# Six products of the identity behind the scores of five levels of a gated recurrence

## The reference

```python
def _hgrn2(q, k, log_f, v, s0):
    ...
    def step(S, inp):
        qc, kc, gc, vc = inp
        b = jnp.cumsum(gc, axis=2)
        diff = jnp.where(tri, b[:, :, :, None, :] - b[:, :, None, :, :], -jnp.inf)
        a = jnp.einsum('bhnmd,bhnd->bhnm', jnp.exp(diff) * kc[:, :, None, :, :], qc)
        o = jnp.einsum('bhnm,bhmv->bhnv', a, vc) + jnp.einsum('bhnd,bhdv->bhnv', qc * jnp.exp(b), S)
        bl = b[:, :, -1:, :]
        S = jnp.exp(bl[:, :, 0, :, None]) * S + jnp.einsum('bhmd,bhmv->bhdv', kc * jnp.exp(bl - b), vc)
        return S, o
    ...
```

## Time and profile before

| | us |
|---|---|
| median of 3 runs (lowest, highest) | 3379.21 (3378.7, 3379.85) |
| the profiled execution, its own time | 3380.08 |
| its span in the trace | 3378.3 |
| TensorE matmul busy in the span | 3088.4 (91%) |
| VectorE, ScalarE, GpSimd busy | 1558.7 (46%), 531.7 (16%), 1058.3 (31%) |
| mean granted TensorE clock | 0.935 of full |

### The profile page before, as it was taken

One profiled execution on the slowest core, in us unless ns is written; L12 is line 12 of the kernel. 1 busy time (PEld: TensorE's weight loads), 2 busy tenths in 40 slices (PEclk: granted clock), 3 DMA queues, 4 the chain that ended last, 5 costly groups with the idle time before them and its releaser, 6 DMA issues. The chain is left out here.

```text
span 3378.3 us, 43932 instructions
## 1 busy us (share of the span) xinstructions
PE 3088.4 (91%) x18135; PEld 2937.9 (87%) x18135; DVE 1558.7 (46%) x1786; ACT 531.7 (16%) x874; POOL 1058.3 (31%) x551
## 2 busy tenths in 40 slices
PE   7997668899999999999988879689979999999999
PEld 6987468789999999998977769469869999999999
DVE  4152454256626436256114444663446634626343
ACT  3111122152000000002111021351252000000000
POOL 3332033114334334343320142103203434434342
PEclk9998679999999999999986789789989999999999
DMA  3111121401111111113100111011221111111112
GB/s 117 44 31 38 24 90 56 142 24 50 45 48 44 39 49 40 47 38 99 41 19 14 46 56 38 15 67 49 87 101 47 48 40 50 37 50 44 44 44 80
DMA packets 274509, 175.86 MB, mean 52 GB/s; under 512 B 15262, under 2 KB 261406, under 8 KB 274398
## 3 DMA queue, kind: packets, MB, share of 16 engines
q1 hardware_dynamic: 274398, 174.29, 16.9%
HBM read 158.00 MB, written 16.27 MB: 52 GB/s over the span
## 5 line engine op out<-in xcount | busy, mean ns | idle before, releaser
L327 PE MATMUL psum<-moving_hi,w_hi 128*128 128x384 f32 (+1 forms) x3888 | 1285.4, 331 | 71.9 <-PEq L515 24.9
L328 PE MATMUL psum<-moving_lo,w_hi 128*128 128x384 f32 (+1 forms) x3888 | 1279.3, 329 | 0.0
L329 PE MATMUL psum<-moving_hi,w_lo 128*128 128x384 f32 (+1 forms) x3888 | 1279.3, 329 | 0.0
L289 POOL TENSOR_TENSOR w_hi<-w_raw,one 128x1024 fp32r<-128x1024 f32 (+2 forms) x236 | 407.1, 1725 | 1934.2 <-PE psum L329 1390.3
L327 PEld LDWEIGHTS psum<-moving_hi,w_hi 128*128 128x128 f32 x3888 | 739.6, 190 | 79.9 <-issue 63.7
L328 PEld LDWEIGHTS psum<-moving_lo,w_hi 128*128 128x128 f32 x3888 | 739.8, 190 | 0.5 <-issue 0.5
L329 PEld LDWEIGHTS psum<-moving_hi,w_lo 128*128 128x128 f32 x3888 | 739.1, 190 | 0.0
L294 POOL TENSOR_TENSOR w_lo<-w_raw,w_hi 128x1024 fp32r<-128x1024 f32 (+2 forms) x236 | 574.0, 2432 | 18.5
L368 DVE TENSOR_TENSOR residual<-psum,residual 128x768 f32 x192 | 130.1, 719 | 491.9 <-PE psum L329 491.2
L327 PE MATMUL psum<-hidden_hi,w_hi 128*128 128x384 f32 (+1 forms) x1056 | 344.6, 326 | 3.2 <-DVE hidden_lo L1900 3.2
L329 PE MATMUL psum<-hidden_hi,w_lo 128*128 128x384 f32 (+1 forms) x1056 | 345.1, 327 | 0.0
(11 more groups left out here) (292 smaller groups left out, 2862.5 us busy)
## 6 DMA issues: line engine op xcount, KB each, us to landing
w_raw<-in_ffn_w_gate SPq DMA_DIRECT2D x44, 512.0 KB, 3.8
w_raw<-in_ffn_w_up SPq DMA_DIRECT2D x44, 512.0 KB, 3.8
w_raw<-in_ffn_w_down SPq DMA_DIRECT2D x48, 384.0 KB, 3.1
w_raw<-in_od_w_in SPq DMA_DIRECT2D x22, 512.0 KB, 3.9
w_raw<-in_ev_w_in SPq DMA_DIRECT2D x20, 512.0 KB, 3.7
w_raw<-in_mem_w_kv SPq DMA_DIRECT2D x16, 512.0 KB, 3.6
work_h<-in_cache_mem_kT SPq DMA_DIRECT2D x4, 2048.0 KB, 12.3
work_h<-in_cache_mem_v SPq DMA_DIRECT2D x4, 2048.0 KB, 17.0
```

The source lines that it names most:

```text
L289: nc.gpsimd.tensor_tensor(hi, raw, ONE.to_broadcast([P, kt * P]), ALU.mult).then_inc(own.sem, 1)
L327: pe.matmul(out, sh, mh, start=(k == 0), stop=False)
L328: pe.matmul(out, sh, ml, start=False, stop=False)
L329: return pe.matmul(out, sl, mh, start=False, stop=(k == kt - 1))
```

## The change

After the scores of a level, and after the signal that VectorE waits for, TensorE computes six products of the identity with its own first 64 columns into bank 2 of PSUM, columns 256 to 319, which nothing reads. This stands at the levels 1 and 4 to 7 of each of the four heads, and not at 2 and 3.

```diff
@@ -2048,6 +2048,9 @@
                         ps = PS[:, lv % 2, j * HALF:(j + 1) * HALF] if j < NBLK else PS[0:S, 2 + lv % 2, 0:S // 2]
                         last = pe.matmul(ps.rearrange("p (b t) -> p b t", t=w // 2), key(h)[:, a:a + m], right_halves(query(h)[:, a:a + m], lv), start=True, stop=True)
                     last.then_inc(scored.sem, 1)
+                    if lv not in (2, 3):
+                        for r in range(6):
+                            pe.matmul(PS[:, 2, 256:320], IDENT[:, :], IDENT[:, 0:64], start=True, stop=True)
 
                 def turn_keys(i):
                     pe.wait_ge(updated.sem, updated.at(8 * i + 8))
```

## The result

The changed kernel takes 3393.66 us (median of 5 runs, 3390.99 to 3398.69) against 3379.85 us for the kernel before beside it (5 runs, 3378.7 to 3380.11): a ratio of 1.0045, 95% interval 1.0032 to 1.0058, or +13.8 us. The forecast was +24.7 us, 3403.9 us, with a range of 3388 to 3418: the sign and the range hold, the middle was 10 us too slow.

What follows compares the result with a forecast made beforehand. Head 0 alternates TensorE and VectorE; from head 1 TensorE's queue bounds. Head 0 +5.3, heads 1 to 3 +23.9, clock giving back 4.5: +24.7 us, 3403.9 us predicted, range 3388 to 3418.

Steps and rivals of the forecast that it cites:

- The price of a block: Each of 20 blocks on TensorE's queue: 12 records, 2.6 us at the low clock, 1.4 us at the full.
- (B): Rival, no change: stationary operand not loaded again, a block costs its streaming only; about 0, 3380 us; chance 0.07.
- (A): Rival, faster: blocks hold the clock up, head 0 turning to full clock by level 5 or 6; 3358 us; chance 0.09.
- the 17.90 us row: Profile stretch 1814.1 to 1832.0 us: TensorE busy without pause yet at 0.50, evidence that the blocks do not lift the clock.
- The list of places where the clock rose: Only after 128-column products standing together: the diagonal with the transposes, or the state products of levels 5 and 6.
- (C): Slower still, the forecast's upper end: blocks thin out 128-column products, all 20 run low; +38.7, 3418 us; within the 0.84.
- The delay: End of the recurrence: a later end passes one to one into the next projection, which still waits some 6 us for POOL.
- The sum by heads: Heads 0 to 3 lengthen by about 5, 8 to 9, 5 to 7 and 5 us; total +24.7 us.
- the pause: Head 0: TensorE idle after levels 1 and 4 to 7, 7.7 us together, taken off 13.0 us of blocks.
- what the clock gives back: Heads 2 and 3: shorter pause after level 7 lets the full clock last into diagonals and transposes; -4.5 us.
- The three items of the term: Full clock in the diagonals of heads 2 and 3, -2.0 and -1.5 us, and the transposes of head 2, -1.0.
- the prediction's three places with gaps: Heads 1 to 3: 0.44 us before level 7's scores; after them 2.11 us (heads 1, 2) or 1.39 us (head 3).

Runs made afterwards that it cites:

- the wide fills: Against the kernel before, without the change's blocks: unread products of 64 to 448 columns where TensorE pauses or has thin work, all heads and tail; 3353.43 us, again 3354.57 us.

## Why the prediction was right, and where it was not

The price of a block was right: 2.55 and 1.34 us against 2.6 and 1.4, 12 records each with a weight load. That the stationary operand is the same each time saved nothing, so (B) falls. That 64 columns would not raise the clock was right: head 0 reads 0.50 at every level, so (A) falls, and the 17.90 us row was the row to go by. The list of places where the clock rose lacks one, though: behind the keys times values of head 1, products of 128 columns too, the clock reads 0.96 from 1809.2 to 1811.3 us. The change did not thin out the dense products so far that all 20 blocks ran low, so (C) falls too. The delay was passed on to the next stage one to one.

The sum by heads was not right. They were to lengthen by about 5, 8 to 9, 5 to 7 and 5 us; they lengthened by 4.0, 4.4, -0.4 and 11.0, and the tail, left out of the sum, by -3.9. That the total stayed in its range is in part luck: heads 1 and 2 and the tail came out far under, and head 3, 6 us over, made up for it. With head 3 as forecast the profile would have some +9, the very edge of the range.

Head 0 was to cost +5.3 us and cost 4.0. The mis-sized term is the pause. I took the idle time that the view shows behind the drawn end of the last matmul, 1.39 us; but records overlap, and a level of 5.06 us with 16 records at a block's spacing (2.55 / 12 = 0.2125 us) has 5.06 - 3.40 = 1.66 us of room. The level with a block lasts 6.02 us (1771.88 to 1777.90), +0.96 and not the +1.2 of the forecast.

The larger miss is the term "what the clock gives back", -4.5 us. With head 0 at 4.0 the blocks at the clocks of before would come to 4.0 + 23.9 = 27.9; the profile has +15.1, so the clock gave back 12.8. The three items of the term came in the size written: the diagonals of heads 2 and 3 took 2.21 us (-1.9 and -1.4), the transposes of head 2 1.20 (-1.0). The reason given, the pause cut to 0.7 us, is not borne out: without the blocks of level 7 the diagonal of head 3 was as fast behind 2.11 us. What was missing: I kept the clock of every other place as it was. In head 1 the block and scores of level 5 ran at the full clock, head 2 went from a mean of 0.65 to 0.80, and the tail ran at 0.88 in place of 0.65 (-3.9 us), with a block after level 7 of head 3 that the sum has at 0; without the blocks of level 7 the tail is at 0.71. Against that, head 3 fell from 0.82 to 0.71, behind a pause that the prediction's three places with gaps leave out: the 1.69 us between the transposes and level 1. Why the clock falls there now and did not before stays open. The mean clock of a stretch is no property of the place: head 1 was at 0.62, 0.69 and 0.80 with nothing changed but the columns of the blocks.

## What to carry to other kernels

Products that nobody reads can bring the full clock, and their width counts: at the same places a low-clock block of 128 columns costs about what one of 16 does on the queue, and the kernel with it is 33.6 us faster. That only made up for the price of the blocks. Faster than before were only the kernels with products of up to 448 columns, put mostly where TensorE waits (behind the diagonal of head 0, during VectorE's update); whether narrow ones would do there was not run, except behind level 7, where they changed nothing. In front of work on a full queue each block costs its 1.3 to 2.6 us. Do not take the clock of a stretch before for its clock after: price the change at both levels. Read the pause from start to start of records, not from the drawn end of the last one.

## What was not expected of the hardware

At the low clock a block of 12 records takes 2.53, 2.55 and 2.67 us with 16, 64 and 128 columns, so the blocks of 128 columns, with which the clock rose in head 0, took almost no more of the queue: the same change gives 3409.8, 3393.7 and 3376.2 us by the width alone.

The first five runs of the kernel before lay within 1.4 us, but the 21 beside the first four experiments spread from 3371.33 to 3384.6 us, the 21 beside the next four from 3363.27 to 3384.81, and the change's own from 3391 to 3398.7. The time goes with the mean granted clock of the run: 0.941 at 3363.27 us, 0.934 at 3384.81. What turns it from run to run is not shown; the two profiles of the wide fills differ by some 3 us in each of the heads 0 and 1. A difference of under 4 us in one head is not told by one profile.
